# Two transformer blocks on one core: rounded passes for the second block's output projection, its weights split among the attention heads, and the rotary angles moved to another engine

## The reference, cut to what matters

```python
# first stack, each layer: six vectors of the conditioning, one wide input projection
mod = c_act @ w_ada[l] + b_ada[l]                   # 1024 -> 6 * 1024
hdn = modulate(rmsnorm(x, norm1_g[l]), shift1, scale1)
proj = hdn @ w_in[l]
q_pe, k_pe = apply_rope(...)                        # angles = positions * inverse frequencies

# second stack, each layer: 4 + 8 + 4 heads, then the output projection
o_fox, o_nsa, o_dil = ...                           # o_nsa has a compressed branch of its own
mix = concatenate([o_fox, o_nsa, o_dil]) @ w_out    # 256 x 1024 by 1024 x 1024
x = x + rms_norm(mix, attn_post_norm[l])
h = rms_norm(x, ffn_pre_norm[l])
x = x + rms_norm(conv_ffn(h, w_up, conv_w, conv_b, w_down), ffn_post_norm[l])
```

## Time and profile before

| | |
|---|---|
| median of 3 runs | 1763.9 us (1763.39 to 1764.46) |
| the profiled execution's own time | 1765.69 us |
| its span | 1764.0 us |
| PE busy | 1697.8 us (96%) |
| PE weight load busy | 1381.1 us (78%) |
| DVE busy | 1180.5 us (67%) |
| ACT busy | 836.3 us (47%) |
| POOL busy | 125.9 us (7%) |
| mean share of the DMA engines | 55.8% |

### The profile page before, as it was taken

The page is one execution under the profiler, slowest core; times in us unless marked ns, Lnnn a source line. Parts: engine busy times, 40 slices in busy tenths (PEclk is TensorE's granted clock), DMA queues, the critical chain, the costliest instruction groups (busy, mean ns, idle before and its releaser), DMA issues. The chain is left out here.

```text
span 1764.0 us, 24759 instructions
## 1 busy us (share of the span) xinstructions
PE 1697.8 (96%) x9275; PEld 1381.1 (78%) x9275; DVE 1180.5 (67%) x2156; ACT 836.3 (47%) x1473; POOL 125.9 (7%) x271
## 2 busy tenths in 40 slices
PE   6899999999999999999999999999999999999998
PEld 3787676589887796774799878766998787669986
DVE  6787555866866875657745675655788766657885
ACT  3335364355443352652455353464554544645552
POOL 1000011000000000210000010141000100410000
PEclk8999999999999999999999999899999999999999
DMA  9787424557854975326465646604665466036652
GB/s 340 273 292 240 144 82 142 181 190 265 298 177 153 351 265 173 120 96 215 144 217 189 193 143 225 169 1 141 206 183 187 158 215 179 1 121 215 187 184 84
DMA packets 185913, 323.71 MB, mean 184 GB/s; under 512 B 13541, under 2 KB 101185, under 8 KB 185793
## 3 DMA queue, kind: packets, MB, share of 16 engines
q1 hardware_dynamic: 183200, 320.54, 55.8%
q10 hardware_dynamic: 2592, 1.57, 0.3%
HBM read 321.02 MB, written 1.05 MB: 183 GB/s over the span
## 5 line engine op out<-in xcount | busy, mean ns | idle before, releaser
L1747 DVE TENSOR_TENSOR ring_r<-ring,high 128x1024 fp32r<-128x1024 f32 (+3 forms) x382 | 450.6, 1195 | 274.3 <-ACT high L1323 265.8
L1323 ACT ACTIVATE high<-ring 128x1024 fp32r<-128x1024 f32 (+3 forms) x382 | 393.0, 1037 | 483.1 <-PE bank L701 345.7
L701 PE MATMUL bank<-ring_r,featT_r 128*128 128x512 f32 (+3 forms) x864 | 330.5, 383 | 0.0
L701 PE MATMUL bank<-high,featT_r 128*128 128x512 f32 (+3 forms) x680 | 265.8, 391 | 7.2 <-DVE ring_r L1747 4.6
L701 PE MATMUL bank<-featT_r,high 128*128 128x256 f32 x960 | 272.6, 284 | 0.0
L701 PE MATMUL bank<-featT_r,ring_r 128*128 128x256 f32 x960 | 271.6, 283 | 0.0
L701 PE MATMUL bank<-oT_r,high 128*128 128x256 f32 x960 | 271.6, 283 | 0.0
L701 PE MATMUL bank<-high,oT_r 128*128 128x512 f32 (+3 forms) x680 | 258.2, 380 | 0.0
L701 PE MATMUL bank<-high,gates_r 128*128 128x512 f32 x736 | 230.0, 390 | 3.4 <-DVE ring_r L1747 2.6
L701 PEld LDWEIGHTS bank<-featT_r,high 128*128 128x128 f32 x960 | 184.2, 192 | 1.0 <-DVE ring_r L1747 0.7
L701 PEld LDWEIGHTS bank<-oT_r,high 128*128 128x128 f32 x960 | 184.2, 192 | 0.3 <-issue 0.2
(11 more groups left out here) (259 smaller groups left out, 2232.9 us busy)
## 6 DMA issues: line engine op xcount, KB each, us to landing
ring<-in_w_ff SPq DMA_DIRECT2D x128, 512.0 KB, 4.8
ring<-in_w_ada SPq DMA_DIRECT2D x96, 512.0 KB, 5.7
ring<-in_w_up SPq DMA_DIRECT2D x176, 256.0 KB, 3.3
ring<-in_w_in SPq DMA_DIRECT2D x64, 464.0 KB, 5.7
ring<-in_w_in SPq DMA_DIRECT2D x48, 512.0 KB, 5.5
ring<-in_w_in SPq DMA_DIRECT2D x48, 474.0 KB, 4.9
ring<-in_w_down SPq DMA_DIRECT2D x44, 512.0 KB, 3.4
ring<-in_w_out SPq DMA_DIRECT2D x24, 512.0 KB, 5.2
```

Of the source, the lines that this page charges most:

```text
L701: ins = pe.matmul(o, a, b, start=start, stop=stop, skip_group_check=True)
L1323: act.activation(it["high"], it["raw"], ACT.Copy).then_inc(high_ready, 1)
L1747: dve.tensor_tensor(it["low"], it["raw"], it["high"].bitcast(F32), ALU.subtract).then_inc(low_ready, 1)
```

## The change

The change has four parts.

1. The output projection of the second stack runs in three rounded passes (`two_as_ready`) instead of plain products. Its eight pieces become split pieces: four high halves go to `high`, four to spare regions (`spare_out_2`). Two pieces are split ahead of the key transposes, the others around the end of the heads.
2. The output of each head pair is split as it leaves PSUM: ACT copies it rounded to `featT_r` at the end of its step, behind the copies to `pT`, and DVE waits for that (`out_high`) and subtracts into `featL`. Before, DVE copied it to `oT` alone.
3. In the compressed branch the transposes of `gel` move from step 0 into the block of key transposes, the remaining pieces of it from ahead of the scores to behind them, and the 16 transposes of `pc` are divided over steps 5 and 6. ACT's copies of these go behind its exponentials.
4. In the first stack, layer 0, `IN_STEPS` is two steps beside every unit instead of 2, 2, 2, 4, 4, 2, ..., so accumulator 9 moves behind the latent projections; the angles are worked out by POOL and ACT's sine moves from unit 2 to unit 5.

```diff
-        IN_STEPS = [[2, 2, 2, 4, 4] + [2] * 5, [0, 4, 4, 4] + [2] * 6]
-        IN_OUT = [{2: 4, 3: 5, 5: 6, 6: 7, 8: 8, 10: 9}, {2: 4, 3: 5, 4: 6, 6: 7, 8: 8, 10: 9}]
+        IN_STEPS = [[2] * 10, [0, 4, 4, 4] + [2] * 6]
+        IN_OUT = [{2: 4, 4: 5, 6: 6, 8: 7, 10: 8}, {2: 4, 3: 5, 4: 6, 6: 7, 8: 8, 10: 9}]
...
+        PAIRS_AT = {5: (0, 2), 6: (1, 3)}
...
+            def angles_of_positions():
+
+                pool.wait_ge(pos_ready, 1)
...
+                for a, ahead in ((1, 0.0), (0, 0.25)):
+                    link(pool.tensor_scalar(turnsn, trig[:, 2, :], 1 / TWO_PI, ahead, ALU.mult, ALU.add))
...
 # PE, second stack
-                turns(key_turns + dil_turns)
-                at_act = [n]
+                turns(key_turns + dil_turns, hidden_back)
...
-                softmax_heads(second_jobs, compressed)
+                softmax_heads(second_jobs, weights_stored, compressed)
                 attention_out.append(made[id(outputs)])
                 pe.wait_ge(outputs.read, made[id(outputs)])
                 deep_tile0.append((made[id(for_dve)], made[id(outputs)]))
-                linear_pair(lambda c, t: oT[:, c, t * P:(t + 1) * P], scaled, (1, 1))
+                two_as_ready({(1, 1, 1): (scaled, 0)}, (for_dve, for_dve, outputs, outputs))
...
 # ACT, softmax_heads
+                    if behind_exps is not None:
+                        behind_exps(i)
+                    if 2 <= i < len(jobs) + 2:
                         for e in range(2):
                             b = tile()
                             copy_out(pT[:, (2 * (i - 2) + e) % NPT, :], b[:, 0:3 * P])
+                    if out0 is not None and i >= 4 and jobs[i - 4]["last"]:
+                        b = outputs_tile(out0)
+                        out0 += 1
+                        act.activation(featT_r[:, jobs[i - 4]["chunk"], :], b[:, 0:S], ACT.Copy).then_inc(out_high, 1)
...
-                softmax_heads(second_jobs, compressed)
+                softmax_heads(second_jobs, compressed, weights_out, attention_out[l] - KD)
+                highs(5)
+                square_banks(deep_tile0[LAYERS1 + 2 * l], (0, 0), (0, 1))
                 highs(2)
-                square_banks(deep_tile0[LAYERS1 + 2 * l], (0, 0), (0, 1))
                 square_parts((0, 0), (0, 1))
...
 # DVE, softmax_heads
-                        read(outputs, dve.tensor_copy(out_view(jobs[i - 4]["chunk"], fill is not None),
-                                                      b[:, 0:S].rearrange("p (t s) -> p t s", t=T)))
...
+                            seen.more(out_high)
+                            read(outputs, dve.tensor_tensor(featL[:, c, :], b[:, 0:S], featT_r[:, c, :].bitcast(F32), ALU.subtract))
...
 # DVE, behind the heads
                 first_quarters(2)
+                split_unit()
                 seen.more(bc_loaded, 32)
                 products(0, 0)
                 normed(0)
                 scale_tokens([0])
-                first_quarters(2)
+                first_quarters(3)
                 features_out(pcol[:, 2 + l, 96:104], None, True, [0])
+                first_quarters(1)
```

More of the change, by code:

```diff
@@ L386, in split, with split_given @@
             return pieces
+        def split_given(*pieces, spare=None):
+            split_units.append(pieces)
+            low_units.append(pieces)
+            for j, it in enumerate(pieces):
+                put(it, spare[j] if spare else None, False, 12)
         def split_together():
@@ L424, in two_blocks @@
                 plain(*[cols_piece(w_uq[l], k0, k0 + 2, (UQ_W * u, UQ_W * u + UQ_W)) for k0 in range(0, QR // P, 2)])
+                for _ in range(0 if l else 2):
+                    ada_piece()
             gate_unit = split(w_in[l], (ATT + 2 * 512, ATT + 3 * 512), later=True)
@@ L461, in two_blocks @@
                 all_k, all_n = slice(0, 2), slice(0, 512)
[L462 to L465, removed]
+                split_given(cols_piece(w, 0, 2, (cols.start, cols.stop), split=True),
+                            *[piece(2, 512, [(slice(0, HD), all_k, all_n, lower[:, j:j + 2, :]),
+                                             (slice(HD, P), all_k, all_n, upper[:, j:j + 2, :])], split=True) for j in (0, 2)],
+                            cols_piece(w, 6, 8, (cols.start, cols.stop), split=True), spare=spare_out_2 if u else None)
             for j in range(CH // 2):
@@ L1160, in _ @@
                     linear((for_dve, for_dve), lambda c, t: lat(6 + c)[:, t * P:(t + 1) * P])
+                if l == 0:
+                    modulation(9)
                 quarters = gate_quarters()
@@ L1262, in compressed @@
                                        full=for_dve.full if h == NSA // 2 - 1 and t else None)
-                    elif i == 5:
-                        seen.more(pc_out)
-                        for h2 in range(NSA // 2):
+                    elif i in PAIRS_AT:
+                        if i == 5:
+                            seen.more(pc_out)
+                        for h2 in PAIRS_AT[i]:
                             b, at_act[0] = claim(for_act)
@@ L1398, in turns_out, with softmax_heads @@
                     read(ins)
-            def softmax_heads(jobs, beside=None):
-                for i in range(len(jobs) + 2):
+            def softmax_heads(jobs, beside=None, behind_exps=None, out0=None):
+                for i in range(len(jobs) + (2 if out0 is None else 4)):
                     if beside is not None:
@@ L2121, in _ @@
                        .then_inc(scaled, 1)
+                if l == 0:
+                    seen.more(sines)
                 kpe = proj[:, :, QR + KVR:SB0].rearrange("p t (h e) -> p t h e", h=1)
@@ L2128, in _ @@
                 features_out(pcol[:, l, 16:24])
+                for _ in range(0 if l else 2):
+                    ada_step()
                 split_unit()
@@ L2135, in _ @@
                     read(for_dve, dve.tensor_copy(qmla[:, 1, u * UQ_W:(u + 1) * UQ_W], b[:, 0:UQ_W]))
+                    for _ in range(2 if u == 0 and l == 0 else 0):
+                        ada_step()
                 for hf in range(2):
```

82 lines of the change are left out of this document (49 added, 33 removed).

## The result

The changed kernel took 1774.52 us (median of 4 runs, 1771.16 to 1775.85) beside 1764.18 us for the kernel before (4 runs, 1763.39 to 1766.73). The ratio is 1.0052, with a 95% interval from 1.0039 to 1.0065: 7 to 11 us slower. The prediction said 1764.0 us, no change that can be told, with a range of 1753 to 1772. The profiled execution took 1775.85 us of its own time, its span is 1774.1 us.

A forecast was written before the change was run, and what follows sets the result against it. PE, busy 96% of the span, was taken as the bound. Per layer -5.8 + 0.55 + 2.4 + 6.0 = +3.1 us, two layers +6.3, with the first stack's -6.2 +0.1 in all: 1764.0 us, range 1753 to 1772.

The forecast's parts named there:

- Term 1: First stack: PE's wait and half clock go, DVE is ready with the rotation slightly later; -6.2 us.
- Term 2: Second stack's projection: three rounded passes cost 0.680 us a product instead of 0.863, 32 products a layer; -5.8 us a layer.
- Term 3: Start of the projection: ACT's copy, then DVE's subtraction, stand between the last output and PE; +0.55 us a layer.
- Term 4: End of the projection: features can't follow the faster products, tile 1's start 36.9 us behind its start; +2.4 us a layer.
- Term 5: Second stack's heads: DVE waits for ACT's output copy, steps 5 and 6 and key transposes lengthen; +6.0 us a layer.
- the clock falls in the new waits: Rival, heads' steps 5 and 6: PE's idle gaps bring half clock, 4 us a layer, 1772 us; chance 0.20.

The follow-up runs named there:

- experiment 1: The kernel before with only part 4 of the change (first stack): 1760.1 us, ratio 0.9971 to the kernel before.
- Kernel 11: 8 with ACT making each output's rounded copy ahead of the step's exponentials instead of behind its copies to pT: 1752.7 us, ratio 0.9928.
- 4: The changed kernel with 7 and 4 plain products doing no useful work in PE's idle time of steps 5 and 6: 1768.9 us, ratio 1.0026.
- 3: The changed kernel with DVE instead of ACT making the rounded copy of each output: 1764.7 us, ratio 1.0000.
- 8: The changed kernel with the compressed branch's order on PE and ACT put back as before, outputs' copies still on ACT: 1762.0 us, ratio 0.9985.
- 6: 3 with the compressed branch's order on PE and ACT put back as in the kernel before: 1757.1 us, ratio 0.9952.
- 5: The changed kernel with the edits of 2 and 3 together: 1759.2 us, ratio 0.9962.
- 2: The changed kernel with compressed weights' transposes and ACT's copies of them ahead of scores and exponentials in steps 5 and 6: 1764.7 us, ratio 1.0001.
- 7: 5 plus products doing no useful work, four in PE's idle time ahead of the heads, four among the narrow compressed scores: 1757.9 us, ratio 0.9971.
- 9: 6 plus products doing no useful work, four in PE's idle time ahead of the heads, four among the narrow compressed scores: 1760.4 us, ratio 0.9970.

## Why the prediction was wrong

- **Term 1, the first stack, was right.** -6.2 predicted, -5.1 measured (experiment 1); the second stack starts 6.4 us earlier in the profile after.
- **Term 2, the passes, was right.** 0.680 us a product predicted, 0.683 measured.
- **Term 3, the start, was right.** PE waits 1.02 us ahead of the first product, 0.53 in the earlier trace rows: +0.5. Kernel 11, whose steps take about as long as those of before (table), has heads 0.5 and 0.7 us longer.
- **Term 4, the end, was right.** Tile 1's features start 36.9 us behind the projection's start, as said. From that start to the next layer's key transposes it took 297.1 us before and 293.5 after: -3.6, where terms 2 and 4 make -3.4.
- **Term 5, the heads, failed.** Together with the start they are 11.9 and 11.6 us longer, 6.5 predicted. The steps were well sized but for the clock: a step with an output takes DVE 4.33 us (4.4 predicted), two with one output 7.5 (7.6), steps 5 and 6 take 6.2 each once the clock is held (6.1). What failed is the cost put on PE's new idle time. The sum counts the waits alone and has no term for the clock, and it gives no reason for that. The rival "the clock falls in the new waits" had it, at 4 us a layer and with a chance of 0.20, and that is what happened: PE stood idle for 3.34 and 1.77 us (2.5 and 2 predicted), and half clock over a further 10.2 and 13.7 us came with it. In steps 5 and 6 it costs 3.8 and 2.3 us (table), and 4 took just these back.
- **The rest that was missing** is for the most part the clock again, at the start of the heads. Up to DVE's first mask of step 4 the heads are 1.9 and 2.6 us longer, 0.6 predicted. In both layers of after, 3.4 us of half clock go with the new wait in the block of key transposes. In layer 0 of 3 the same wait stands and the clock held. PE's first scores, of after and then of 3:

```profile
1123.51 2.93 PE L739 MATMUL bank<-wide,qz 128*128 128x128 f32 x8 [1.81 <-ACT gates L1359]
```

```profile
1120.65 1.58 PE L739 MATMUL bank<-wide,qz 128*128 128x128 f32 x8 [1.80 <-ACT gates L1359]
```

  From the first key transpose to the first mask it is 4.32 us before, 4.88 in 3 and 5.60 after. So the wait costs 0.6, as predicted, and the clock the rest. With 6.1 us for steps 5 and 6 and 3.3 for what is missing ahead of step 4, the sum would be 1773.4 us, beside 1774.5 measured.
- **The cause of the waits** is shown from both sides. The output's copy behind `pT` costs 2.9 us a layer in the old order by the ratios (8 against 6), and 5.0 against 11, where ACT still makes the copy. The new order costs another 5.9 (after against 8), of which the clock in the gaps has 2 to 3 (after against 4). The parts don't add exactly, since the same idle time is in several (5 against 2 and 3).
- **Left open:** how the time would be with the new order kept and only ACT's copy early. It wasn't tried. Nor were the rounded projection alone, and the narrow products or the gap ahead of them filled each by itself.

## What to carry to other kernels

Where one engine hands a small result to another, its place in the giver's queue can cost more than the operation: here 16 copies of 0.37 us, 6 us of work, cost 10 us by their place. Put such a copy ahead of what waits for the receiver. When a sum has PE idle for 2 to 3 us in a place that was dense, count what follows at half clock in the same sum and not as a rival. And when a change has four parts, time the parts: here the first stack was worth 5 us, the rounded projection some 7 (its 3.6 us a layer in the traces), and the order of ACT's copies in the heads hid both.

## What the runs showed of the hardware

- PE can be busy without a break and still lose its clock. In the kernel after, the 5 us ahead of the fall at 1133 are full of scores and of the 32 products with 15 columns. (PE had stood idle for 1.81 us some 10 us ahead of the fall.)

```profile
1128.00:1133.00 5.00, 5.00 (x42) 4.75 (x41) 3.99 (x23) 2.53 (x12) 1.34 (x3) 1.00 0.87 265
```

  Every kernel here has half clock for 10.2 us or more behind these, but for 7 (3.4 in both layers) and 9 (6.8 in layer 0), which had products of 256 columns among them and in the gap ahead. Which of the two fillings held the clock isn't shown.
- Identical code starts the second stack at different times. From experiment 2 on all kernels are the same up to there, and their first key transposes of layer 0 stand between 1116.7 and 1122.0 us. One profile's start of the second stack is therefore known to 2 or 3 us only; the ratios of several runs had to decide on term 1.
